# Mamba-2 SSD mixer: one masked matrix per head for both scan directions

## The reference

```
seg = cum[:, :, None] - cum[:, None, :]
decay = jnp.exp(jnp.where(mask, seg, -jnp.inf))
cb = jnp.einsum('bign,bjgn->bijg', cc, bc)
w = cb[..., None] * decay * dtc[:, None]
y = jnp.einsum('bijgr,bjgrp->bigrp', w, xc)
y = y + jnp.einsum('bign,bgrpn->bigrp', cc, state) * jnp.exp(cum)[..., None]
```

## Time and profile before

| | us |
|---|---|
| median of 3 runs (2547.65 to 2548.4) | 2547.81 |
| the profiled execution | 2548.42 |
| its span in the trace | 2546.7 |
| TensorE busy | 2263.1 |
| VectorE busy | 1510.4 |
| ScalarE busy | 1104.1 |
| GpSimd busy | 277.3 |

### The profile page before, as it was taken

How to read it: one execution, slowest core, us unless ns; L and a number is a source line. 1 busy time by engine, 2 the same in 40 slices (tenths; PEclk the granted TensorE clock), 3 DMA queues, 4 the chain that set the end, 5 groups by cost and what they waited for, 6 DMA issues and landing times. The chain is left out here.

```text
span 2546.7 us, 26247 instructions
## 1 busy us (share of the span) xinstructions
PE 2263.1 (89%) x9262; PEld 1471.1 (58%) x9262; DVE 1510.4 (59%) x1347; ACT 1104.1 (43%) x918; POOL 277.3 (11%) x180
## 2 busy tenths in 40 slices
PE   5799979979794699999769999999999999999981
PEld 2455545646552544447546666666676666666651
DVE  2323331564647400000368889888989998998874
ACT  3322212231404100000147677767777777777661
POOL 0000011141414200000001101110111011011100
PEclk8899979989896699999779999999999999999996
DMA  6111012132212242211349999999999999999964
GB/s 175 36 50 50 16 66 83 50 116 70 96 66 99 76 149 79 69 66 66 110 171 358 362 359 360 369 357 358 360 365 357 360 356 365 360 358 365 358 237 176
DMA packets 159813, 528.33 MB, mean 207 GB/s; under 512 B 15414, under 2 KB 81368, under 8 KB 123864
## 3 DMA queue, kind: packets, MB, share of 16 engines
q1 hardware_dynamic: 152376, 505.96, 53.6%
q0 software_dynamic: 7392, 21.77, 2.6%
HBM read 510.77 MB, written 21.10 MB: 209 GB/s over the span
## 5 line engine op out<-in xcount | busy, mean ns | idle before, releaser
L1607 DVE TENSOR_TENSOR w_low<-weights,w_high 128x2048 fp32r<-128x2048 f32 x384 | 873.4, 2289 | 122.5 <-ACT w_high L1601 116.5
L1601 ACT ACTIVATE w_high<-weights 128x2048 fp32r<-128x2048 f32 x384 | 735.5, 1917 | 336.6 <-PE ps L1696 230.3
L1696 PE MATMUL ps<-w_high,rows_high 128*96 128x512 f32 x1024 | 405.4, 396 | 1.1 <-DVE w_low L1607 1.1
L1696 PE MATMUL ps<-w_high,rows_low 128*96 128x512 f32 x1024 | 403.5, 394 | 0.0
L1696 PE MATMUL ps<-w_low,rows_high 128*96 128x512 f32 x1024 | 402.7, 393 | 0.0
L1754 PE MATMUL ps<-w_high,act_high 128*96 128x512 f32 x512 | 206.6, 403 | 30.0 <-DVE w_low L1607 30.0
L1696 PEld LDWEIGHTS ps<-w_high,rows_low 128*96 128x96 f32 x1024 | 165.8, 162 | 71.7
L1696 PEld LDWEIGHTS ps<-w_high,rows_high 128*96 128x96 f32 x1024 | 165.9, 162 | 71.2 <-DVE w_low L1607 2.3
L1696 PEld LDWEIGHTS ps<-w_low,rows_high 128*96 128x96 f32 x1024 | 166.1, 162 | 69.6
L1754 PE MATMUL ps<-w_high,act_low 128*96 128x512 f32 x512 | 201.9, 394 | 0.0
L1754 PE MATMUL ps<-w_low,act_high 128*96 128x512 f32 x512 | 201.0, 393 | 0.0
(11 more groups left out here) (288 smaller groups left out, 2625.9 us busy)
## 6 DMA issues: line engine op xcount, KB each, us to landing
weights<-in_w SPq DMA_DIRECT2D x384, 1024.0 KB, 5.7
weights<-in_w_in SPq DMA_DIRECT2D x32, 1024.0 KB, 5.3
weights<-in_w_in SPq DMA_DIRECT2D x16, 512.0 KB, 5.0
temps<-cum_rows SPq DMA_DIRECT2D x8, 1024.0 KB, 6.9
weights<-cum_rows SPq DMA_DIRECT2D x8, 1024.0 KB, 11.0
weights<-in_w_up_ssd SPq DMA_DIRECT2D x8, 1024.0 KB, 6.1
weights<-expert_rows SPq DMA_DIRECT2D x16, 512.0 KB, 9.6
ssd_out_T<-temps SPq DMA_DIRECT2D x4, 1024.0 KB, 3.9
```

Of the source, the lines that this page charges most:

```text
L1601: nc.scalar.activation(w_hi[:, split_at(it, j)], slot(at, 1)[:, 0, :], ACT.Copy).then_inc(w_hi_ok, 1)
L1607: nc.vector.tensor_tensor(w_lo[:, split_at(it, j)], slot(at, 1)[:, 0, :], w_hi[:, split_at(it, j)].bitcast(F32), ALU.subtract).then_inc(w_ ...
L1696: last = nc.tensor.matmul(ps[0:CAP, n, :], a[:, k, :], w[:, cols], start=False, stop=k == UP - 1 and i == 2)
```

## The change

One matrix for each head serves both directions. In the head, ln dt (of dt not less than 1e-37) is subtracted from `cum_n`, after its other readers, so that GpSimd's subtraction gives cum_i - cum_j + ln dt_j. In the group, `copy_predicated` puts the forward exponent over the backward one where the lower-triangle mask is set; one Exp; one product with cb, read from PSUM; and 8 matmuls a tile with plain x. On the diagonal this holds the forward share alone; the backward share, cb_ii * dtb_i, is added to D (`x_gain`), which GpSimd multiplies with x instead of D.

```diff
+LEAST = 1e-37
...
                 nc.scalar.activation(l_, u_, ACT.Ln).then_inc(dt_a, 1)
+                act.wait_ge(dt_v, 9)
+                nc.scalar.activation(l_, r_, ACT.Ln).then_inc(ln_dt, 1)
...
+                nc.vector.tensor_scalar(r_, dt_n, LEAST, None, ALU.max).then_inc(dt_v, 1)
                 v.wait_ge(cum_ps, 1)
...
                 nc.vector.tensor_tensor(dend_n, dend_n, dt_n, ALU.mult).then_inc(cum_v, 1)
+                v.wait_ge(ln_dt, 1)
+                nc.vector.tensor_tensor(cum_n, cum_n, l_, ALU.subtract).then_inc(cum_v, 1)
...
-        x_dt = [[take(GW) for _ in range(2)], s_st]
+        in_w = [take(GW) for _ in range(2)]
...
-        m_w = [[a[:, d * HPG * P:(d + 1) * HPG * P].rearrange("p (h i) -> p h i", h=HPG) for d in range(2)]
-               for a in (take(UNIT), weights[:, 0:UNIT])]
-        cb_m = [take(SEQ).rearrange("p (t i) -> p t i", t=NT) for _ in range(2)]
+        m_w = [take(HPG * P).rearrange("p (h i) -> p h i", h=HPG) for _ in range(2)]
+        cb_d = take(SEQ).rearrange("p (t i) -> p t i", t=NT)
+        cb_diag = take(NT)
+        x_gain = take(NT * HPG).rearrange("p (t h) -> p t h", t=NT)
...
             for t in range(NT):
-                pe.wait_ge(m_ok, g * 8 + 2 * t + 2)
-                pe.wait_ge(xdt_ok, g * 8 + 2 * t + 2)
+                pe.wait_ge(m_ok, g * 4 + t + 1)
...
                 for h in range(HPG):
-                    for d in range(2):
-                        last = nc.tensor.matmul(ps[:, 4 + t % 2, h * HD:(h + 1) * HD], m_w[t % 2][d][:, h, :],
-                                                x_dt[t % 2][d][:, h * HD:(h + 1) * HD], start=d == 0, stop=d == 1)
+                    last = nc.tensor.matmul(ps[:, 4 + t % 2, h * HD:(h + 1) * HD], m_w[t % 2][:, h, :],
+                                            x_n[:, t, h * HD:(h + 1) * HD], start=True, stop=True)
...
-                            pe.wait_ge(cb_ok, g * 2 + 2)
+                            pe.wait_ge(m_ok, g * 4 + 4)
...
-                e = cum_bc[t][:, 0]
+                e = cum_bc[t][:, 1]
                 nc.scalar.activation(e, e, ACT.Exp).then_inc(seg_exp, 1)
...
+                if t == 0:
+                    pool.wait_ge(diag_ok, g + 1)
                 alone(pool)
-                dh = d_bc[:, bass.ds(g * HPG, HPG)].unsqueeze(2).broadcast_to([P, HPG, HD])
+                dh = x_gain[:, t, :].unsqueeze(2).broadcast_to([P, HPG, HD])
...
-                nc.vector.tensor_tensor(b[:, 0], b[:, 0], b[:, 1], ALU.min).then_inc(seg_min, 1)
+                alone(v)
+                nc.vector.copy_predicated(b[:, 1], low[:].unsqueeze(1).broadcast_to([P, HPG, P]).bitcast(U32), b[:, 0]).then_inc(seg_min, 1)
...
             seg_least(0)
-            x_by_dt(0)
             v.wait_ge(cb_ps, g + 1)
-            for d, m in ((0, low), (1, high)):
-                nc.vector.tensor_tensor(cb_m[d], ps[:, 3, :].rearrange("p (t i) -> p t i", t=NT),
-                                        m[:].unsqueeze(1).broadcast_to([P, NT, P]), ALU.mult).then_inc(cb_ok, 1)
+            cb = ps[:, 3, :].rearrange("p (t i) -> p t i", t=NT)
+            nc.vector.tensor_tensor(cb_d, cb, ident[:].unsqueeze(1).broadcast_to([P, NT, P]), ALU.mult).then_inc(cb_ok, 1)
+            v.wait_ge(cb_ok, g * 3 + 1)
+            nc.vector.tensor_reduce(cb_diag, cb_d, AX.X, ALU.add).then_inc(cb_ok, 1)
+            v.wait_ge(cb_ok, g * 3 + 2)
+            nc.vector.tensor_tensor(x_gain, dt_n[:, :, bass.ds(g * HPG + SH, HPG)], cb_diag.unsqueeze(2).broadcast_to([P, NT, HPG]),
+                                    ALU.mult).then_inc(cb_ok, 1)
+            v.wait_ge(cb_ok, g * 3 + 3)
+            nc.vector.tensor_tensor(x_gain, x_gain, d_bc[:, bass.ds(g * HPG, HPG)].unsqueeze(1).broadcast_to([P, NT, HPG]),
+                                    ALU.add).then_inc(diag_ok, 1)
             for t in range(NT):
                 if t + 1 < NT:
                     seg_least(t + 1)
                 v.wait_ge(seg_exp, g * 4 + t + 1)
-                v.wait_ge(cb_ok, g * 2 + 2)
                 if t >= 2:
                     v.wait_ge(yi_ps, g * 4 + t - 1)
-                for d in range(2):
-                    nc.vector.tensor_tensor(m_w[t % 2][d], cum_bc[t][:, 0], cb_m[d][:, t, :].unsqueeze(1).broadcast_to([P, HPG, P]),
-                                            ALU.mult).then_inc(m_ok, 1)
-                if t + 1 < NT:
-                    x_by_dt(t + 1)
+                nc.vector.tensor_tensor(m_w[t % 2], cum_bc[t][:, 1], cb[:, t, :].unsqueeze(1).broadcast_to([P, HPG, P]),
+                                        ALU.mult).then_inc(m_ok, 1)
                 if t:
                     y_begin(t - 1)
```

More of the change, by code:

```diff
@@ L163, in build @@
         dt_a = sem("dt_a")
+        ln_dt = sem("ln_dt")
         dt_v = sem("dt_v")
@@ L775, in build @@
         m_ok = sem("m_ok")
-        xdt_ok = sem("xdt_ok")
+        diag_ok = sem("diag_ok")
         xd_ok = sem("xd_ok")
@@ L808, in build @@
                   (take(UNIT), take(UNIT), weights[:, UNIT:2 * UNIT], weights[:, 2 * UNIT:3 * UNIT])]
-        m_w = [[a[:, d * HPG * P:(d + 1) * HPG * P].rearrange("p (h i) -> p h i", h=HPG) for d in range(2)]
-               for a in (take(UNIT), weights[:, 0:UNIT])]
-        cb_m = [take(SEQ).rearrange("p (t i) -> p t i", t=NT) for _ in range(2)]
+        m_w = [take(HPG * P).rearrange("p (h i) -> p h i", h=HPG) for _ in range(2)]
+        cb_d = take(SEQ).rearrange("p (t i) -> p t i", t=NT)
+        cb_diag = take(NT)
+        x_gain = take(NT * HPG).rearrange("p (t h) -> p t h", t=NT)
         x_D = x_e
-        in_w = x_dt[0]
         cvp = take(CTG * (TAPS + 1)).rearrange("p (k c) -> p k c", c=CTG)
@@ L1052, in seg_least @@
                 b = cum_bc[t]
-                nc.vector.tensor_tensor(b[:, 0], b[:, 0], b[:, 1], ALU.min).then_inc(seg_min, 1)
[L1055 to L1058, removed]
-                for d in range(2):
-                    nc.vector.tensor_tensor(by_head(x_dt[t % 2][d]), by_head(x_n[:, t, :]), per_head(DT, t, g, d), ALU.mult).then_inc(xdt_ok, 1)
+                alone(v)
+                nc.vector.copy_predicated(b[:, 1], low[:].unsqueeze(1).broadcast_to([P, HPG, P]).bitcast(U32), b[:, 0]).then_inc(seg_min, 1)
             def y_begin(t):
@@ L1136, in load_group @@
             if not (isinstance(g, int) and g == 1):
-                sp.wait_ge(m_ok, g * 8 - 8)
+                sp.wait_ge(m_ok, g * 4 - 4)
                 load_cum(sp, g - 1)
@@ L1154, in _ @@
                     store_y(sp, g - 2)
-                sp.wait_ge(m_ok, 8 * (GR - 1))
+                sp.wait_ge(m_ok, 4 * (GR - 1))
                 load_cum(sp, GR - 1)
```

## The result

The changed kernel takes 2508.93 us (median of 4 runs, 2508.23 to 2509.66) against 2547.73 us (4 runs, 2547.13 to 2548.4) of the kernel before beside it: ratio 0.9848, 95% interval 0.9831 to 0.9865. The gain is 38.8 us.

The account below looks back on a forecast made before the run. The prediction took TensorE, through the tile matmuls L906, to bound all four SSD groups; 22.1 us (groups 0 to 2) plus 13.0 (last group) is 35.1, off 2548.42 gives 2513.3, stated as 2513, range 2510 to 2518.5.

Parts of the forecast that it names:

- (a): SSD groups 0 to 2: L906 goes from 16 to 8 matmuls a tile, gaining 3 x 7.36 = 22.1 us.
- (b): VectorE, per tile: drops three products, worth nothing in groups 0 to 2; copy_predicated 1.3 us, product from PSUM 1.22 us.
- (c): GpSimd beside VectorE: the PSUM product is not slowed; copy_predicated can be, by up to 0.86 us each time.
- (d): Diagonal: its chain takes 1.8 us against 1.2 in the last group; GpSimd waits for it; cost nothing in groups 0 to 2.
- (e): Last group, instruction by instruction: 12.7 us gained, 14.2 with no port waits, 13.0 taken.
- (f): Head of the kernel: three small added instructions are covered by waits, taken as 0; without that cover 1.1 us.
- (g): Queues and later stages: nothing becomes late, and the shift passes unchanged from the SSD block to the end.
- VectorE setting the last group's pace: Rival, chance 0.10: copy_predicated takes 2.4 us and enters the last group's chain; gain 30.7 us, time 2517.7.
- The clock did not rise within L911: Rival, chance 0.05: the clock rises within the last group's tile matmuls, ending them 3 us earlier; time 2510.
- nor fall more often: Rival, chance 0.06: clock dips in all groups, 1.5 us x 3, and a late rise in the last; 2519 to 2520.
- The very slow copy: Rival, chance 0.03: copy_predicated ahead of every product makes the kernel slower; at 8 us each the time is 2562.

Follow-up runs that it names:

- rep_before: The unedited kernel before, run and traced a second time: 2547.47 us, ratio 0.9997.
- rep_after: The changed kernel, unedited, run and traced a second time: 2509.88 us, ratio 0.9842.
- double_matmuls: The changed kernel with each of the tile matmuls issued twice into the same sum: 2547.06 us, ratio 0.9989.
- half_matmuls: The kernel before with only one direction's matmul for each head, VectorE's work and the waits kept: 2516.7 us, ratio 0.9868.
- pool_early: The changed kernel with GpSimd multiplying x by D alone, without waiting for the diagonal: 2510.17 us, ratio 0.9843.
- late_mix: The changed kernel with three idle 128x64 matmuls ahead of the stage behind SSD, so the merge begins 1.3 us later: 2512.41 us, ratio 0.986.
- copy_twice: The changed kernel with each copy_predicated done twice, same result: 2516.87 us, ratio 0.9867.
- warm_last: The changed kernel with five idle 128x512 matmuls in the last group between cb and the first tile: 2509.27 us, ratio 0.984.

## Why the prediction was right, and where it was wrong

**(a) L906 halved in groups 0 to 2: right.** 22.1 us were forecast; the three comparable pairs (before and after, rep_before and rep_after, double_matmuls and after) give 22.8, 19.7 and 20.8. half_matmuls and double_matmuls show that it is TensorE's time. The 3.1 us between the first two pairs are mostly the dips of the clock in the kernel before, which the prediction had priced at 1.5 us each: 1.5 and 1.3 us between before and rep_before.

**(b), (c) VectorE's durations: right.** 1.31 us for the copy (taken: 1.3), 1.21 for the product (1.22), 2.08 us for a copy beside GpSimd (2.1); a product from PSUM was never slowed.

**(d) The diagonal: right in its cost, nothing.** Its chain takes 2.1 us (795.14 to 797.23) instead of 1.8. pool_early shows that GpSimd's wait costs nothing.

**(e) The last group: mis-sized, by 0.6 to 1.4 us.** Taken were 13.0 us; it is 14.4 (13.8 and 13.6 in the other pairs), near the 14.2 with no port waits. Three parts of the working did not come about. The first is the port wait of 0.8 us for tile 1's copy: it began at 797.27, 0.15 us before GpSimd's x product, and took 1.30. The second is the start of the diagonal: it began 18.83 us after the group's start, where L1071 had begun 19.39 after it: the matmuls for cb (L894, now L901) took 1.30 us instead of 1.85. That part is luck of the clock and not the change's, since rep_before and half_matmuls, which have the old VectorE program, took 1.29 and 1.32. The third is the late product of tile 2: the prediction has it 0.7 us behind TensorE; it was done at 806.5, in time for a third block at 806.7 (799.73 plus two of 3.48).

**(f) The head: right.** The first start in all other traces lies at 435.0 to 437.4 whatever the edit, so its 0.6 us between the first two profiles is scatter.

**(g) "After the SSD block each stage starts from a barrier, so the shift passes to the end": this is the step that failed.** Nothing outside the SSD groups was to change. It does in all three pairs: of 39.6, 36.3 and 38.0 us between the spans, 2.4, 2.8 and 3.6 lie outside the groups' 37.2, 33.5 and 34.4. In the pair of rep_before 2.7 us of them, and in that of double_matmuls 2.9, are between merge and experts, where the kernel after has the fast router and those two the slow one; late_mix shows that a merge begun 1.3 us later makes the router 3.1 us longer. In the first pair both routers are of the fast kind, and what is outside the SSD groups is 0.6 us in the head, 0.2 at the end of the SSD block, 0.3 between merge and experts, and 1.4 in the closing stage, where the last scatter to the end takes 50.5 us in before and 48.8 to 50.0 in the other traces. No edit here reaches that stage, and what makes it vary was not tried. The forecast of 35.1 us lies among the SSD groups' own gains of 33.5 to 37.2; with (e) at 14.4 the sum would have been 36.5 and the time 2512, inside the range. The rest of the way to 2508.9 is outside the block, which the range gave no width. What sets the kind in the kernel before from one execution to the next, and what its runs of up to 2552.75 us are, stays open: no trace of such a run was taken.

**The rivals.** VectorE setting the last group's pace came true only where it was brought about, in copy_twice, half_matmuls and the first tiles of warm_last. The clock did not rise within L911 (0.50 at 800 to 803 us), nor fall more often (first state step 1.98, 3.40 and 3.65 us in groups 0 to 2 of after; 1.98, 3.44 and 3.78 before). The Trainium skill, "TensorE: Matmul & The Clock Gate", section "What's actually happening", has sustained busyness release the throttle; 13.9 gapless us of L911, and 27.6 in double_matmuls, do not agree. The very slow copy is excluded by 1.31 us.

## What to carry to other kernels

Halve the work of an engine only where a timeline shows that its own end is waited for, and then look for the one stretch without cover (here the last group), since there the other engine's saving decides how much is kept. Ask what runs on GpSimd beside VectorE's products with both inputs in SBUF: moving that, and the loads it waits for, added no instruction to it and brought 24 us more. Give a range some width for the stages that the edit doesn't touch, when TensorE's clock changes level in them, and take a second trace of the kernel before: here its clock alone moved the SSD groups by over 3 us.

## What the runs showed of the hardware

- The same four gate products took 9.26 us beside GpSimd's subtractions and 2.50 us without them; the norm's four (tensor_scalar, one tensor input) 5.84 and 1.67 us; two x_e products 3.75 and 1.28 us; a copy_predicated 2.08 and 1.31 us. The product with PSUM as one input took 1.19 to 1.22 us either way. The Trainium skill, "SBUF — State Buffer", section "SBUF: two separate sides", says that VectorE and GpSimd share a pair of ports that one instruction holds for its whole length, and that VectorE needs it when it has two inputs in SBUF; the gate, x_e and PSUM rows agree; the norm's were slowed with one tensor input.
- The clock kept 2.4 GHz through two tiles of 128x64 matmuls after five 128x512 ones (warm_last: 1.00 in 800 to 803 us, 0.95 in 803 to 806), and was at 0.50 from 806 on, before the third. Without the five, TensorE idle for 4.62 us ahead of the tiles, it was 1.00 in 796 to 797, 0.50 in 798 to 799.7 and 0.50 through all four tiles (after). It rose in cb's 128x128 matmuls of the last group, from 0.50 (793.8 to 794.2) to 0.94 (794.2 to 794.7), while 13.9 (after) and 27.6 us (double_matmuls) of gapless 128x64 ones did not raise it.
- The router's 96 passes take 15.9 us or 19.0 us, with the instructions the same, by the granted clock (0.72 or 0.55 over the first 32). In late_mix 1.3 us at the start of the merge decided it; the slow kind also comes without the three small matmuls (half_matmuls, double_matmuls, copy_twice). That the moment of the start decides fits the seven traces listed under late_mix, and was not tried by itself.
- The kernel before, traced twice, differs by 3.6 us in its SSD groups, with the same instructions: four passes of L926 3.44 or 1.98 us, a piece of 16 passes 8.34 or 7.03, cb's eight 1.85 or 1.29.
